# Value transposes and key-query products of a linear attention moved to two other PSUM banks and ahead of each level's projection

## The reference, cut to what matters

```
proj = h @ w_in
qkv = jax.nn.silu(causal_depthwise_conv(proj[..., :QKV_W], conv_w))
z = proj[..., QKV_W:QKV_W + V_W].reshape(b_, s_, LA_HEADS, LA_DV)
...
a = jnp.where(strict, a, 0.0) + jnp.eye(CHUNK, dtype=f32)
rhs = jnp.concatenate([v_beta, k_beta * jnp.exp(g)[..., None]], axis=-1)
sol = lax.linalg.triangular_solve(a, rhs, left_side=True, lower=True, unit_diagonal=True)
u, w = sol[..., :dv], sol[..., dv:]
attn_intra = jnp.einsum('bhncd,bhnsd->bhncs', q, k) * decay
```

## Time and profile before

| | |
|---|---|
| median of 3 runs | 1662.47 us |
| lowest and highest | 1659.87 and 1666.7 us |
| the profiled execution's own time | 1671.45 us |
| its span, from the first to the last instruction | 1669.6 us |
| mean granted TensorE clock over the span | 0.970 |
| TensorE busy | 1596.1 us, 96% of the span |
| VectorE busy | 1172.9 us, 70% |
| ScalarE busy | 896.9 us, 54% |
| the four projections, three turns and levels 4 to 6 with their transposes and products, 119.48 to 197.96 us | 78.48 us |

### The profile page before, as it was taken

One profiled execution on the slowest core, in us unless ns is written; L12 is line 12 of the kernel. 1 busy time (PEld: TensorE's weight loads), 2 busy tenths in 40 slices (PEclk: granted clock), 3 DMA queues, 4 the chain that ended last, 5 costly groups with the idle time before them and its releaser, 6 DMA issues.

```text
span 1669.6 us, 20426 instructions
## 1 busy us (share of the span) xinstructions
PE 1596.1 (96%) x8056; PEld 1334.9 (80%) x8056; DVE 1172.9 (70%) x1094; ACT 896.9 (54%) x825; POOL 48.2 (3%) x37
## 2 busy tenths in 40 slices
PE   7998998999998878899999999999999999999998
PEld 6897875999995464788888888888888888888886
DVE  4865225544453244498898898889889889889885
ACT  1422222433440152477677767767677677677764
POOL 0000000000001100000000000000000000000000
PEclk9998898999999968799999999999999999999999
DMA  7211146545545402399999999999999999999990
GB/s 252 101 51 51 51 173 233 200 172 184 202 174 181 151 1 97 139 371 382 350 369 382 346 377 382 344 370 381 350 371 373 356 373 373 355 369 378 348 382 32
DMA packets 184958, 439.30 MB, mean 263 GB/s; under 512 B 5325, under 2 KB 5477, under 8 KB 184896
## 3 DMA queue, kind: packets, MB, share of 16 engines
q1 hardware_dynamic: 182528, 430.52, 70.4%
q0 software_dynamic: 2368, 7.91, 1.4%
HBM read 436.29 MB, written 2.65 MB: 263 GB/s over the span
## 4 chain that ended last, share of the span: by engine, by line
PE 95%; DVE 3%; ACT 1%; POOL 0%; issue 0%; DMA 0%; SPq 0%; DVEq 0%; POOLq 0%; ACTq 0%
PE bank L1060 12%; PE bank L1062 12%; PE bank L1061 12%; PE bank L621 7%; PE bank L1047 6%; PE bank L1045 6%; PE bank L1046 6%; PE bank L561 5%; PE bank L848 3%; PE bank L850 3%; PE bank L849 3%; PE bank L954 2%; PE bank L798 2%; PE bank L870 2%; PE bank L830 2%; PE bank L831 2%
## 5 line engine op out<-in xcount | busy, mean ns | idle before, releaser
L1763 DVE TENSOR_TENSOR ring_r<-ring,buf_r 128x2048 fp32r<-128x2048 f32 x336 | 751.1, 2285 | 29.5 <-ACT buf_r L1292 29.5
L1292 ACT ACTIVATE buf_r<-ring 128x2048 fp32r<-128x2048 f32 x336 | 629.4, 1914 | 49.5 <-PE bank L1047 43.4
L1060 PE MATMUL bank<-ring_r,buf_r 128*128 128x512 f32 x896 | 354.9, 396 | 1.6 <-DVE buf_r L1858 1.6
L1062 PE MATMUL bank<-buf_r,buf_r 128*128 128x512 f32 x896 | 349.7, 390 | 0.0
L1061 PE MATMUL bank<-buf_r,buf_r 128*128 128x512 f32 x896 | 349.0, 390 | 0.0
L1062 PEld LDWEIGHTS bank<-buf_r,buf_r 128*128 128x128 f32 x896 | 168.2, 188 | 36.0
L1060 PEld LDWEIGHTS bank<-ring_r,buf_r 128*128 128x128 f32 x896 | 168.4, 188 | 34.7 <-DVE buf_r L1858 1.7
L1061 PEld LDWEIGHTS bank<-buf_r,buf_r 128*128 128x128 f32 x896 | 168.5, 188 | 33.4
L1045 PE MATMUL bank<-ring_r,buf_r 128*128 128x512 f32 x448 | 175.9, 393 | 0.0
L1047 PE MATMUL bank<-buf_r,buf_r 128*128 128x512 f32 x448 | 174.6, 390 | 0.0
L1046 PE MATMUL bank<-buf_r,buf_r 128*128 128x512 f32 x448 | 174.3, 389 | 0.0
(11 more groups left out here) (256 smaller groups left out, 1674.5 us busy)
## 6 DMA issues: line engine op xcount, KB each, us to landing
ring<-in_moe_w_gate SPq DMA_DIRECT2D x56, 2048.0 KB, 8.5
ring<-in_moe_w_up SPq DMA_DIRECT2D x56, 2048.0 KB, 8.5
ring<-in_moe_w_down SPq DMA_DIRECT2D x56, 2048.0 KB, 8.3
ring<-in_a_w_in SPq DMA_DIRECT2D x8, 2048.0 KB, 8.7
ring<-in_dense_w_gate SPq DMA_DIRECT2D x7, 2048.0 KB, 8.7
ring<-in_dense_w_up SPq DMA_DIRECT2D x7, 2048.0 KB, 9.1
ring<-in_dense_w_down SPq DMA_DIRECT2D x7, 2048.0 KB, 7.9
ring<-in_a_w_out SPq DMA_DIRECT2D x2, 2048.0 KB, 7.8
```

Source lines behind the costliest of these rows:

```text
L1060: pe.matmul(o, xh, low[:, c], start=k == 0, stop=False)
L1062: ins = pe.matmul(o, xh, high[:, c], start=False, stop=k == KT - 1)
L1292: act.activation(HB[m % NHB], half_words(m, U_MOE), ACT.Copy).then_inc(m_wh, 1)
L1763: dve.tensor_tensor(half_low(m, U_MOE), half_words(m, U_MOE), HB[m % NHB], ALU.subtract).then_inc(m_wl, 1)
```

## The change

The value transposes and the key-query products go to banks 2 and 3 (`2 + t`, the second chunk of a pair in bank 3), which hold groups 2 and 3 of `y` and of the turns. On TensorE they stand ahead of `project(6 + lv)` instead of behind it. Of their waits `fill_free` is gone; in its place the turns of levels 3 to 5 wait ahead of groups 2 and 3 until VectorE has emptied those banks, and the wait for all four `attn` stands ahead of L748 instead of behind `project(13)`. On VectorE `values` and `attn` stand ahead of the level's `conv` instead of behind it. `FILLS` loses its "v" and "a" entries.

```diff
-FILLS = ([("p", f) for f in range(4, 10)] + [("v", 0), ("v", 1), ("p", 10), ("v", 2), ("v", 3), ("p", 11), ("a", 0),
-         ("a", 1), ("p", 12), ("a", 2), ("a", 3), ("s", 0), ("p", 13), ("p", 14), ("p", 15)])
+FILLS = [("p", f) for f in range(4, 13)] + [("s", 0), ("p", 13), ("p", 14), ("p", 15)]
...
             def value_tokens(g):
-                fill_free("v", g)
                 pe.wait_ge(silu_done, 6 + 2 * half)
...
-                    m = transpose(quad(fill_bank("v", g), i), CONV[:, 2 * HEADS + 4 * half + i, tok(t)])
+                    m = transpose(quad(2 + t, i), CONV[:, 2 * HEADS + 4 * half + i, tok(t)])
...
             def attn(g):
-                fill_free("a", g)
                 pe.wait_ge(silu_done, 10 + 2 * half)
...
-                    m = pe.matmul(quad(fill_bank("a", g), i), CONV[:, HEADS + hd, tok(t)], CONV[:, hd, tok(t)],
+                    m = pe.matmul(quad(2 + t, i), CONV[:, HEADS + hd, tok(t)], CONV[:, hd, tok(t)],
...
             def turn(lv):
                 for g in range(4):
                     pe.wait_ge(u_ready, 4 * lv + g + 1)
+                    if g >= 2 and lv in (3, 4):
+                        pe.wait_ge(vt_ready, 2 * lv - 7 + g)
+                    if g >= 2 and lv == 5:
+                        pe.wait_ge(attn_ready, g - 1)
...
-                project(6 + lv)
                 if lv in (3, 4):
                     for g in (2 * lv - 6, 2 * lv - 5):
                         value_tokens(g)
                 if lv >= 5:
                     for g in (2 * lv - 10, 2 * lv - 9):
                         attn(g)
+                project(6 + lv)
...
             pe.wait_ge(u_ready, 4 * NLEV)
+            pe.wait_ge(attn_ready, 4)
...
             project(13)
-            pe.wait_ge(attn_ready, 4)
...
             level(3)
-            conv(9)
             dve.wait_ge(pow_out, powers[0])
             for g in range(2):
                 values(g)
+            conv(9)
             mask(0)
             mask(1)
             level(4)
-            conv(10)
             for g in range(2, 4):
                 values(g)
+            conv(10)
             mask(2)
             mask(3)
             level(5)
-            conv(11)
             for g in range(2):
                 attn(g)
+            conv(11)
```

More of the change, by code:

```diff
@@ L601, in fill_free @@
                     pe.wait_ge(z_done, f - N_Z + 1)
[L602 to L605, removed]
                 else:
@@ L1547, in values @@
                 dve.wait_ge(vt_tp, g + 1)
-                dve.tensor_tensor(R[2][:, quads(g), :], as_quad(fill_bank("v", g)), bc(inv[:, col(g):col(g) + 4], P),
+                dve.tensor_tensor(R[2][:, quads(g), :], as_quad(2 + g % 2), bc(inv[:, col(g):col(g) + 4], P),
                                   ALU.mult).then_inc(vt_ready, 1)
@@ L1555, in attn @@
                 dve.wait_ge(gq_mm, g + 1)
-                dve.tensor_tensor(R[0][:, quads(g), :], as_quad(fill_bank("a", g)), X[2][:, quads(g), :], ALU.mult
+                dve.tensor_tensor(R[0][:, quads(g), :], as_quad(2 + g % 2), X[2][:, quads(g), :], ALU.mult
                                   ).then_inc(attn_ready, 1)
```

## The result

The changed kernel took 1655.95 us (median of 8 runs, 1647.49 to 1661.21) and the kernel before, run beside it, 1669.34 us (8 runs, 1659.87 to 1673.27). The ratio is 0.9917, with an interval of 0.9894 to 0.9939: by the ratio 13.9 us less, with an interval of 10.2 to 17.7, where 17.4 were forecast, and faster by more than 0.5%. The time lies 2 us above the range of the prediction. Two things need keeping apart: the gain, of which the forecast is 3.5 us above the measured value and just inside the interval, and the kernel before, which had shown a median of 1662.47 us over three runs and shows one of 1669.34 over eight.

What follows compares the result with a forecast made beforehand. TensorE was taken as the bound, busy 96% of the span. Waits of 9.30 us and clock loss of 8.20 us, taken as 17.4, off the median 1662.47 gave 1645.1 us, range 1639 to 1654.

Steps and rivals of the forecast that it cites:

- The removed waits, 9.30 us: TensorE's three waits for VectorE's convolution, ahead of value transposes and a key-query product, would go: 3.25 + 3.25 + 2.80 us.
- The clock behind the breaks, 8.20 us: Slow clock in turn, `y` and `z` after each break, 1.94, 3.06 and 3.20 us, all taken as gone.
- undisturbed prices: Full-clock lengths of the work behind a break, from level 2: 9.85 us after the first two, 10.03 after the third.
- two ways: Waits plus clock loss, and the whole stretch of 78.48 us less 61.04 without breaks; both taken as 17.4 us.
- The absolute time, 1645.1 us: The gain of 17.4 us applied to the earlier runs' median of 1662.47 us, a ratio of 0.9895.
- What moved on VectorE, and who is late next: `values` ahead of `conv(9)` costs nothing, 5.5 us to spare in the turn; 1.1 us remain before the next level's subtraction.
- The wait for `attn` ahead of L748, `project(13)` behind `z_out(12)`, the loads: Both waits near the output projections cost nothing; weight loads move ahead with TensorE's stream, so the gain isn't lost.
- The rival that VectorE or ScalarE would be late: VectorE late ahead of the next level, 2.4 us in each of three levels; gain only 6 to 10 us; chance 0.10.
- That the stream would lose its clock: The unbroken stretch's work running at about double price, time about 1706 us, slower; chance 0.04.
- That nothing is gained: Gain hidden by a later stage, or banks 2 and 3 holding TensorE in the turn; about 1662 us; chance 0.08.
- The signs to look for: In the trace: no TensorE wait from 119 to 190 us, clock 1.00, one-column matmuls at about 180.5, everything behind 17 us earlier.
- That the fall behind them may grow or stay away: The clock fall behind the one-column matmuls of L741, 1.6 us, may grow or stay away; used for the range.

Runs made afterwards that it cites:

- e3: The kernel before, with transposes that nobody reads (28, 28 and 24) filling TensorE's three breaks; median 1665.65 us, ratio 0.9984 to the kernel before.
- e4: The changed kernel with VectorE's old order, `values` and `attn` behind the level's `conv` again; median 1666.51 us, ratio 1.0012 to the kernel before.
- e1: The kernel before, unchanged, run and profiled once more; ratio 1.0009 against the runs of the kernel before beside it.
- e11: The changed kernel, unchanged, profiled once more; 65.13 us in the compared stretch, 1474.9 us from the one-column matmuls to the end.
- e12: The changed kernel, unchanged, another profile; 65.13 us in the compared stretch, 1464.7 us from the one-column matmuls to the end.
- e7: The changed kernel with the one-column and 16-column matmuls spread between matmuls of `project(12)` and `project(1)`; median 1656.20 us, ratio 0.9925 to the kernel before.
- e5: The changed kernel's order on TensorE and VectorE, but in the old shared banks 6 and 7; median 1659.72 us, ratio 0.9955 to the kernel before.

## Why the prediction was right and wrong, by its own steps

- *The removed waits, 9.30 us:* right. They are gone, they were 9.3 us in each of six profiles, and e3 against the changed kernel, 75.17 - 65.13 = 10.0 us, is this term and the 0.7 us around the waits, without any clock loss.
- *The clock behind the breaks, 8.20 us:* the mechanism is right and the size is wrong. It is this term of the gain that failed. The loss is real (it is in all six profiles of before, in none of the six of the change, and e4 brings it back), but its mean over six profiles is 3.7 us, and 4.4 with the 0.8 us around the waits that the prediction counted as clock. The prediction read one execution and took it for the price. Even for that execution 8.20 was too much, since its undisturbed prices (9.85 and 10.03) are short by that 0.8: its granted clocks gave 7.5, and the stretches at 1.00 give 7.4. That its two ways agree at 17.4 is no check of this, since both use the same prices. It did name the bound ("the clock loss is that of one execution") and used it for the range alone, not for the value. With 4.4 the sum is 13.7 us, and 13.9 were measured. That the gain was forecast too large rests on these profiles; the timed runs alone, 10.2 to 17.7 us, don't exclude 17.4.
- *The absolute time, 1645.1 us:* this step failed too, and it is the larger part of the miss. The prediction subtracted its gain from 1662.47, the median of three runs; eight runs have 1669.34. That is 6.9 of the 10.9 us between 1645.1 and 1655.95, and with the measured base the range would have been 1646 to 1661 us and would have held the time. The profiled execution's 1671.45 us stood 9 us above the median of three, and the prediction took it for an unusual one. In its time it was near the usual one: 30 runs beside e1 have a median of 1669.14. With the measured median as base the forecast of 17.4 us would have been 1651.9. The three runs' own spread of 6.8 us, nearly half the gain, was the warning.
- *What moved on VectorE, and who is late next:* right, 5.7 us and 1.36 us of spare where 5.5 and 1.1 were forecast. e4 shows that the first one is bought by VectorE's order alone.
- *The wait for `attn` ahead of L748, `project(13)` behind `z_out(12)`, the loads:* right, no wait of TensorE there. The output projection starts 12.8 us earlier (226.2 against 239.0), less than the 17 that were to be seen, since the start and the one-column matmuls were slower in this profile.
- *The rival that VectorE or ScalarE would be late:* did not come. *That the stream would lose its clock:* did not come; 1.00 over 130 us, and 1.00 over the length in all six profiles. *That nothing is gained:* did not come, and e4 is what it would have looked like: a wait of 3.5 us in the turn.
- *The signs to look for:* the one-column matmuls, forecast at about 180.5 us of the chain, are at 180.57 in e11 and 180.36 in e12; in the profile above they are at 183.62, since its start was 3.1 us slower than that of before. *That the fall behind them may grow or stay away:* both came, 10.39 us above and none in e4.

What stays open: whether the falls of the clock outside the stretch are on average the same in both kernels (6.6 us apart by the profiles, nothing by the timed runs), why a break is followed by a fall in one execution and not in the next, and what the spread narrow matmuls of e7 are worth.

## What to carry to other kernels

Where two kinds of work share a pair of buffers in turn, look who emptied the buffer last and what stands ahead of the emptying on that engine: here 9.3 us of waits went, and with two short VectorE instructions behind a convolution the new banks had 10.6 us of them again. A break in TensorE's stream of some 3 us costs its own length each time, and up to as much again by the clock, but that second price is drawn anew in each execution: take it as a range, from several profiles. And compare a gain with the spread of the runs before trusting a base: three runs of a kernel whose times spread over 15 us say little about its median.

## What the runs showed of the hardware

The clock's share differs between executions of one kernel, and the time with it. Over its 12 timed runs e1 had spans of 1660 us at a mean granted clock of 0.978 up to 1672 us at 0.970, and the changed kernel of 1645.6 us at 0.979 up to 1659.4 at 0.968: 1.2 to 1.5 us for each thousandth of mean clock, with the same instructions. The three breaks of 1.6 us and less in e5 (one profile) cost no clock; breaks of 2.8 to 3.6 us cost from nothing (the second in e1) to 3.0 us. And TensorE's clock fell while TensorE was busy: behind 32 passes of one column in each of the twelve profiles of the two kernels (0.67 in 183.62 to 194.01), though not in e4 (1.00), and in some behind 32 passes of 16 columns (0.75 in 22.96 to 36.78); "TensorE: Matmul & The Clock Gate" of the Trainium skill, section "What's actually happening", says that the clock gate follows how busy the engine has been. Read as the profile's busy time this doesn't hold here: that stretch has 10.39 us busy of 10.39.
